# Transposing gathered rows one unit sooner, gathers ahead of scatters, column transfers in stage 3, and another order for the row tiles of a final norm

## The reference, cut to what matters

```
h = rmsnorm(x, norm_ffn_g) * (1 + sc2) + sh2
aff = softmax(h @ w_router)                       # 16 experts
gate, idx = top_k(aff.T, cap)                     # cap = 2 T / 16: 256 latent and 32 context tokens
xs = h[idx]
y  = (silu(xs @ w_e_gate[e]) * (xs @ w_e_up[e])) @ w_e_down[e]     # 1024 wide, per expert
x += gt2 * scatter_add(y * gate)
y_prompt, y_sample = rmsnorm(x, norm_final_g)
```

## Time and profile before

| what | value |
|---|---|
| median of 3 runs | 2752.36 us (2743.16 to 2754.95) |
| the profiled execution | 2750.49 us |
| its span, first to last instruction | 2748.7 us |
| TensorE matmuls busy | 2464.9 us, 90% |
| DVE, ACT, POOL busy | 59%, 44%, 28% |
| mean granted TensorE clock | 0.924 of full |
| chain that ended last | PE 63%, DVE 10%, ACT 9%, issue 6%, DMA 3% |
| start of expert 1 and of expert 14 on TensorE | 1529.6 and 2541.46 us |

### The profile page before, as it was taken

The page is one execution under the profiler, slowest core; times in us unless marked ns, Lnnn a source line. Parts: engine busy times, 40 slices in busy tenths (PEclk is TensorE's granted clock), DMA queues, the critical chain, the costliest instruction groups (busy, mean ns, idle before and its releaser), DMA issues.

```text
span 2748.7 us, 41035 instructions
## 1 busy us (share of the span) xinstructions
PE 2464.9 (90%) x15405; PEld 2165.3 (79%) x15405; DVE 1633.1 (59%) x2729; ACT 1214.1 (44%) x1952; POOL 762.4 (28%) x686
## 2 busy tenths in 40 slices
PE   5579999999997888999549999999999999999886
PEld 2568878687885567667219999999999999999886
DVE  1576959497694443341364666665566666655485
ACT  3555453455423223323115455555444555555473
POOL 1020110102000021101012544444445544444443
PEclk9889989999997888889659999999999999999998
DMA  5875465656637433422644666656666666566793
GB/s 204 301 271 184 165 227 191 230 184 210 203 110 239 136 112 126 147 83 99 108 99 140 200 190 187 184 182 200 203 192 200 202 180 190 181 193 198 248 311 149
DMA packets 287075, 505.63 MB, mean 184 GB/s; under 512 B 31614, under 2 KB 230107, under 8 KB 271098
## 3 DMA queue, kind: packets, MB, share of 16 engines
q1 hardware_dynamic: 247562, 377.84, 41.9%
q0 software_dynamic: 39408, 126.38, 16.4%
HBM read 405.63 MB, written 98.53 MB: 183 GB/s over the span
## 4 chain that ended last, share of the span: by engine, by line
PE 63%; DVE 10%; ACT 9%; issue 6%; DMA 3%; POOL 2%; DVEq 0%; SPq 0%; ACTq 0%; POOLq 0%
PE bank L1405 18%; PE bank L1407 17%; PE bank L1406 17%; DVE hl_exp L2372 2%; ACT hl_exp L1021 2%; ACT work_exp L1037 2%; DVE work_exp L2382 2%; PE bank L1588 1%; PE bank L1526 1%; PE bank L1619 1%; PE bank L1654 1%; PE bank L1553 1%; DVE work_out L2061 1%; PE bank L1565 1%; DMA raw_exp<-in_w_mod_dram 1%
## 5 line engine op out<-in xcount | busy, mean ns | idle before, releaser
L1405 PE MATMUL bank<-act_hl_exp,hl_exp 128*128 128x288 f32 x3072 | 914.7, 298 | 59.6 <-POOL act_hl_exp L1335 24.5
L1406 PE MATMUL bank<-act_hl_exp,hl_exp 128*128 128x288 f32 x3072 | 909.7, 296 | 0.0
L1407 PE MATMUL bank<-act_hl_exp,hl_exp 128*128 128x288 f32 x3072 | 908.0, 296 | 0.0
L1405 PEld LDWEIGHTS bank<-act_hl_exp,hl_exp 128*128 128x128 f32 x3072 | 579.5, 189 | 66.4 <-issue 46.9
L1407 PEld LDWEIGHTS bank<-act_hl_exp,hl_exp 128*128 128x128 f32 x3072 | 581.7, 189 | 0.0
L1406 PEld LDWEIGHTS bank<-act_hl_exp,hl_exp 128*128 128x128 f32 x3072 | 580.5, 189 | 0.0
L2372 DVE TENSOR_TENSOR hl_exp<-work_exp,hl_exp 128x1024 fp32r<-128x1024 f32 x192 | 237.3, 1256 | 224.1 <-ACT hl_exp L1021 223.9
L2372 DVE TENSOR_TENSOR hl_exp<-raw_exp,hl_exp 128x1024 fp32r<-128x1024 f32 x192 | 237.4, 1253 | 200.9 <-ACT hl_exp L1021 200.9
L2014 DVE SCALAR_TENSOR_TENSOR work_proj<-work_proj,wcv 128x392 f32<-128x392 f32 (+11 forms) x600 | 343.1, 642 | 0.0
L1356 POOL DMA_INDIRECT x_rows<-work_exp x135 | 253.0, 1874 | 141.7 <-DVE work_exp L2403 105.2
L1021 ACT ACTIVATE hl_exp<-work_exp 128x1024 fp32r<-128x1024 f32 x192 | 199.3, 1054 | 191.2 <-PE bank L1407 191.2
(11 more groups left out here) (320 smaller groups left out, 3669.8 us busy)
## 6 DMA issues: line engine op xcount, KB each, us to landing
hl_proj<-park_w POOLq DMA_DIRECT2D x80, 1024.0 KB, 5.5
raw_exp<-in_w_e_gate_dram SPq DMA_DIRECT2D x32, 1024.0 KB, 5.7
raw_exp<-in_w_e_up_dram SPq DMA_DIRECT2D x32, 1024.0 KB, 5.7
work_exp<-in_w_e_gate_dram SPq DMA_DIRECT2D x32, 1024.0 KB
work_exp<-in_w_e_up_dram SPq DMA_DIRECT2D x32, 1024.0 KB, 7.6
raw_exp<-in_w_e_down_dram SPq DMA_DIRECT2D x32, 1024.0 KB, 5.7
work_exp<-in_w_e_down_dram SPq DMA_DIRECT2D x32, 1024.0 KB, 5.4
park_w<-hl_proj SPq DMA_DIRECT2D x10, 2048.0 KB, 12.1
```

The costliest lines, as they stand in the source:

```text
L1405: pe.matmul(out, lh, rh, start=first, stop=False)
L1406: pe.matmul(out, lh, rl, start=False, stop=False)
L1407: return pe.matmul(out, ll, rh, start=False, stop=last_)
```

## The change

It has five parts.

- Stage 3's SP program issues the four column transfers after the first tile of block m = 2; they are gone from the start of routing.
- In an expert, gather_T and modulate_xe of column groups 0 to 7 stand in units 6 to 9; xe_hi stays in units 7 to 10, ahead of that unit's modulate_xe. gate_cols goes ahead of elo in unit 0.
- POOL's order in an expert is gather(e+2), scatter(e), xe_lo(e+2). In experts 13 and 14, outside the loop, a scatter waits for one block of out_rows at a time, and expert 13's scatter stays ahead of the gather.
- TensorE's units 0 and 1 wait for one transpose per bank, not two per unit.
- Final norm: rows are asked for after units 8 and 9; squares, roots, normalising and stores get other units; tiles 10 to 17 are loaded after expert 14's scatter has landed, come after the three `fix` tiles in the order (place), and are stored after the fixed rows have been scattered.

```diff
+        FIX, LAST = 10, NTILE + 3
+        def place(t):
+            return t if t < FIX else t + 3
...
+        f_s3 = Sig(k_m, 0, 0, 33)
...
                 if m > 0:
                     tile_out(G3[m] - 1)
+                if m == 2:
+                    for i, cols in ((1, A2), (2, mod[:, 24:32, :])):
+                        for cnd in range(2):
+                            sp.dma_start(mod_d[i, cnd].rearrange("(k p) -> p k", p=128), cols[:, :, cnd],
+                                         allow_slow_non_contiguous=True).then_inc(e_mod.sem, 16)
...
-            for i, cols in ((1, A2), (2, mod[:, 24:32, :])):
-                for cnd in range(2):
-                    sp.dma_start(mod_d[i, cnd].rearrange("(k p) -> p k", p=128), cols[:, :, cnd],
-                                 allow_slow_non_contiguous=True).then_inc(e_mod.sem, 16)
...
             def load_again(n):
-                sp.wait_ge(f_st[n % 2], 32 * (n // 2 + 1))
+                if n == 0:
+                    sp.wait_ge(e_sc, 16 * NB * (NE - 1))
+                if n % 2 == 0:
+                    sp.wait_ge(f_st[n // 2], 64)
...
+            STORE_AT = {15: (0,), 17: (1,), 18: (2, 3), 19: (4,), 20: (5, 6), 21: (7,), 22: (8, 9)}
             for u in range(2 * NEXP):
                 expert_units(NE - 2 + u // NEXP, range(u % NEXP, u % NEXP + 1))
-                if u in (7, 8):
-                    load_rows(u - 7)
-                if 12 <= u < 16:
-                    load_again(u - 12)
-                if 11 <= u < 16:
-                    store_pair(u - 11)
+                if u in (8, 9):
+                    load_rows(u - 8)
+                for t in STORE_AT.get(u, ()):
+                    store_tile(t)
                 if 19 <= u < 23:
-                    store_pair(u - 14)
+                    load_again(u - 19)
...
-            for q in range(2):
-                sp.wait_ge(f_st[q], STORED[q])
+            sp.wait_ge(f_wr, 48)
+            for t in range(FIX, NTILE):
+                store_tile(t)
+            upto(sp, f_s3, 16 * (NTILE - 8))
...
+            SQUARES_AT = {7: (0, 1), 8: (1, 3), 9: (3, 5), 10: (5, 6), 11: (8, 10), 18: (10, 12), 19: (12, 14), 20: (14, 18)}
+            ROOTS_AT = {9: (0, 5), 11: (5, 10), 19: (10, 14), 20: (14, 18)}
...
                     if 7 <= j < 11 and not last:
                         for k in (2 * (j - 7), 2 * (j - 7) + 1):
+                            xe_hi(e + 1, k)
+                    if 6 <= j < 10 and not last:
+                        for k in (2 * (j - 6), 2 * (j - 6) + 1):
                             modulate_xe(e + 1, k)
-                        for k in (2 * (j - 7), 2 * (j - 7) + 1):
-                            xe_hi(e + 1, k)
...
+            def gather_next(e, n_ids):
+                pool.wait_ge(e_gat, 16 * NB * e + 16 * NB)
+                pool.wait_ge(e_xk, 8 * e + 8)
+                pool.wait_ge(e_gate, e + 1)
+                gather(e + 1, n_ids)
+
+            def scatter(e, n_ids):
                 wait_pos(pool, e_sc, 16 * NB * e)
...
+                if isinstance(e, int):
+                    for n in range(2 if e == NE - 2 else 0):
                         upto(pool, f_x[n], 16 * (LOADS[n + 1] - LOADS[n]) + (16 if n == 0 else 0))
+                else:
+                    wait_alone(pool, s_alone, e_yev, NB * e + NB)
                 for b in range(NB):
+                    if isinstance(e, int):
+                        pool.wait_ge(e_yev, NB * e + b + 1)
...
+            gather_next(0, 1)
+            next_lo(0)
             with pool.Fori(0, NE - 3) as i:
-                expert(i + 1, False)
-            expert(NE - 2, False)
+                gather_next(i + 1, 2 * i + 2)
+                scatter(i, 2 * i + 3)
+                next_lo(i + 1)
+            scatter(NE - 3, 2 * NE - 4)
+            gather_next(NE - 2, 2 * NE - 3)
+            next_lo(NE - 2)
+            scatter(NE - 2, 2 * NE - 2)
...
-                                pe.wait_ge(e_yt, 8 * before + (2 * j + 2))
+                                pe.wait_ge(e_yt, 8 * before + (2 * j + q + 1))
...
-            NORM_PAIR = {6: 0, 7: 1, 8: 2, 9: 3, 10: 4, 13: 5, 14: 6, 15: 7, 16: 8}
+            TILES_AT = {10: (0,), 12: (1,), 13: (2, 3), 14: (4,), 15: (5, 6), 16: (7,), 17: (8, 9), 20: (10, 11), 21: (12, 13),
+                        22: (14, 15, 16), 23: (17,)}
...
+                    if j == 0:
+                        gate_cols(e)
                     if more and j != 7 and j != 11:
                         elo(e, j + 2)
-                    if j == 0:
-                        gate_cols(e)
...
-                    if 7 <= j < 11 and not last_e:
-                        gather_T(e + 1, 2 * (j - 7))
-                        gather_T(e + 1, 2 * (j - 7) + 1)
+                    if 6 <= j < 10 and not last_e:
+                        gather_T(e + 1, 2 * (j - 6))
+                        gather_T(e + 1, 2 * (j - 6) + 1)
+                    for t in TILES_AT.get(u + j, ()) if u is not None else ():
+                        norm_rows(place(t), 128, row_tile(t))
```

More of the change, by code:

```diff
@@ L1063, in squares @@
                 for t in range(t0, t1):
-                    square(t, 128, row_tile(t), 0, D, sq6[:, t:t + 1])
+                    c = place(t)
+                    square(c, 128, row_tile(t), 0, D, sq6[:, c:c + 1])
             def roots(t0, t1):
-                upto(act, f_sq, t1)
-                act.activation(rt6[:, t0:t1], sq6[:, t0:t1], ACT.Sqrt, bias=eps[:, :],
-                               scale=1.0 / D).then_inc(f_rt.sem, t1 - t0)
-            def norms(at):
-                if at in (4, 5):
-                    squares(3 * at - 12, 3 * at - 9)
-                if at == 5:
-                    roots(0, 6)
-                if at in (6, 7):
-                    squares(2 * at - 6, 2 * at - 4)
-                if at == 7:
-                    roots(6, 10)
-                if 11 <= at < 15:
-                    squares(2 * at - 12, 2 * at - 10)
-                if at == 12:
-                    roots(10, 14)
-                if at == 14:
-                    roots(14, 18)
+                a, z = place(t0), place(t1 - 1) + 1
+                upto(act, f_sq, z)
+                act.activation(rt6[:, a:z], sq6[:, a:z], ACT.Sqrt, bias=eps[:, :], scale=1.0 / D).then_inc(f_rt.sem, z - a)
+            SQUARES_AT = {7: (0, 1), 8: (1, 3), 9: (3, 5), 10: (5, 6), 11: (8, 10), 18: (10, 12), 19: (12, 14), 20: (14, 18)}
+            ROOTS_AT = {9: (0, 5), 11: (5, 10), 19: (10, 14), 20: (14, 18)}
+            def norms(at):
                 if at == 17:
@@ L1089, in norms @@
                     fix_roots()
+                if at in SQUARES_AT:
+                    squares(*SQUARES_AT[at])
+                if at == 10:
+                    squares(6, 8)
+                if at in ROOTS_AT:
+                    roots(*ROOTS_AT[at])
             def fix_squares():
@@ L1093, in fix_squares @@
                 for i, n in ROWS:
-                    t = NTILE + i
-                    square(t, n, fix[:, i, :], 0, D, sq6[0:n, t:t + 1])
+                    c = FIX + i
+                    square(c, n, fix[:, i, :], 0, D, sq6[0:n, c:c + 1])
             def fix_roots():
                 for i, n in ROWS:
-                    t = NTILE + i
-                    upto(act, f_sq, t + 1)
-                    act.activation(rt6[0:n, t:t + 1], sq6[0:n, t:t + 1], ACT.Sqrt, bias=eps[0:n, :],
+                    c = FIX + i
+                    upto(act, f_sq, c + 1)
+                    act.activation(rt6[0:n, c:c + 1], sq6[0:n, c:c + 1], ACT.Sqrt, bias=eps[0:n, :],
                                    scale=1.0 / D).then_inc(f_rt.sem, 1)
@@ L1336, in xe_lo, with next_lo @@
                     .then_inc(e_xlo, 1)
-            def expert(e, last):
-                if not last:
-                    pool.wait_ge(e_gat, 16 * NB * e + 16 * NB)
-                    pool.wait_ge(e_xk, 8 * e + 8)
-                    pool.wait_ge(e_gate, e + 1)
-                    gather(e + 1, 2 * e + 1)
-                    for k in range(KC):
-                        xe_lo(e + 1, k)
-                if last:
-                    return
+            def gather_next(e, n_ids):
[4 more added lines that the diff above has]
+            def scatter(e, n_ids):
                 wait_pos(pool, e_sc, 16 * NB * e)
                 pool.tensor_copy(ids_s[:, :], ids[:, e, :]).then_inc(e_ids, 1)
-                wait_alone(pool, s_alone, e_ids, 2 * e + 2)
-                if isinstance(e, int) and e == NE - 2:
-                    for n in range(4):
+                wait_alone(pool, s_alone, e_ids, n_ids)
+                if isinstance(e, int):
+                    for n in range(2 if e == NE - 2 else 0):
                         upto(pool, f_x[n], 16 * (LOADS[n + 1] - LOADS[n]) + (16 if n == 0 else 0))
-                wait_alone(pool, s_alone, e_yev, NB * e + NB)
+                else:
+                    wait_alone(pool, s_alone, e_yev, NB * e + NB)
```

(5 more changed lines are left out.)

25 lines of the change are left out of this document (10 added, 15 removed).

## The result

Two results have to be told apart. Where the change was timed first (call that chip A; its number is not on record) the kernel before took 2747.76 us in the median of its 4 runs and the changed one 2711.96 us (2708.22 to 2719.40), a ratio of 0.9867 [0.9841, 0.9893]; the forecast was 2707, with 2693 to 2722. Where both were run once more at the end (chip D) the changed kernel took 2743.56 us (12 runs) against 2751.43 (29 runs): 0.9984 [0.9963, 1.0004], no change that can be measured, and outside the range of the forecast. The first profile is read here; what chip D shows comes with its experiment.

What follows compares the result with a forecast made beforehand. TensorE, busy nine tenths of the span, was taken as the bound, so only its standing time could be saved; 2750.49 - 11.3 - 15.3 - 19.0 = 2704.9, plus 1.9 to the median of runs, gave 2707 us, range 2693 to 2722.

Steps and rivals of the forecast that it cites:

- Part 1, the columns: Start of routing: moving the column transfers to stage 3 ends TensorE's wait for the first w_mod block, -11.3 us.
- Part 2, the boundaries: Boundaries between experts: earlier gather_T and modulate_xe remove TensorE's 1.09 us loss at fourteen boundaries, -15.3 us.
- the finer wait: TensorE at expert boundaries: waiting for one transpose, not two, gives 0.36 us that nothing needs any more.
- so no cost of the branch shows: Expert loop: the gap is 0.94 us with the branch and 0.93 past the loop's end, so no branch cost.
- The rival that takes the branch: Expert loop: the branch keeps the gap, at most 1.09 us twelve times, +13.1, 2720 us; chance 0.14.
- Part 3, POOL: POOL in each expert: gathers before scatters, with 10 us of cover before xe_lo is due; price 0.
- Part 4, expert 14: Expert 14: rows asked for earlier end ACT's 15.11 us wait; 83.95 us instead of 103.0, -19.0 us.
- The four steps of the 7.2 us: End of expert 14: late ehi(12), elo, one tile and a transpose start expert 15 6.5 us late; slower clock adds 0.7.
- Part 5, expert 15 and the tail: Expert 15 and tail: moved stores and row loads cost 0, staying 77.6 and 26.6 us; bounds 0 and +15.
- 8 us more than the loads take: Expert 15: weights behind SP's wait for expert 14's scatter are wanted 42 us in, leaving 8 us of cover.
- the DMA engines bound expert 15: Rival in expert 15: row tiles, stores and weights fill the DMA engines, 2715 to 2722 us; chance 0.18.
- The slower rival, POOL falling behind: Every expert: scatters ending past T+54.7 delay xe_lo and the next expert, time over 2766 us; chance 0.03.

## Why the prediction was right, and where it was not

On chip A the time lies in the range and most of the mechanisms are those laid out. On chip D the time, 2743.56 us, lies outside it, by the step named under part 2.

- *Part 1, the columns (-11.3).* Right: the wait for w_mod is gone, some 10.5 us by the kernel that moves them alone, and stage 3 pays nothing that can be told from its own spread, some 14 us between executions.
- *Part 2, the boundaries (14 x 1.09 = -15.3).* Right on chips A and B, and for the reason given: ehis 5.82 us apart instead of 6.65 (6.07 was laid out), no wait for the output transposes, 1.21 us an expert. That the finer wait is needed by nothing was right too. On chips C and D the step failed, in this sentence: the gap is 0.94 with the branch and 0.93 past the loop's end, "so no cost of the branch shows". Equal gaps said only that no cost shows while TensorE pauses there. The rival that takes the branch had one thing right, that the time would be lost in the twelve passes entered by the jump, but not the place in the pass nor the size. It took 1.09 us a pass as the most that could be hidden and made it 2720; in the traces it is 14.7 us over twelve passes on chip C and 27.7 on D. That the branch is the cause is not shown.
- *Part 3, POOL (0).* Right: with the old order the time is the same.
- *Part 4, expert 14 (-19.0: 83.95 us).* Right: expert 14 took 82.6 us. The four steps of the 7.2 us are all in the timeline: the late ehi(12), elo, the tile, one transpose. But the gain does not reach the end, since expert 15 takes it back: with the row tiles in their old order the whole expert stage is as long.
- *Part 5, expert 15 and the tail (0, up to +15).* This is the term that was mis-sized on every chip: +14.3 and +1.8 us on chip A. By the starts of expert 15's 576 matmuls in the two traces the 14.3 can be named: 7.6 us more in gaps between them, the four waits for converted weights; 2.9 us by 28 more matmuls that start 0.24 us apart and not 0.133, the lower of TensorE's two clock levels, which came after the two longest of these waits (granted clock 0.83 from 2660 to 2680); and 3.7 us by which the last transposes ended later behind the last matmul, since six row tiles stood in front of them. The step put "8 us more than the loads take" as cover behind the wait for the scatter; the wait that decides is another, that of SP for the landing of tile 7's store, 18.7 us, with the last weights and the last rows behind it. The rival "the DMA engines bound expert 15" had the right place, about the right price (+8 to +15) and part of the reason: the store takes so long while the DMA engines are full (share 1.00 from 2630 to 2647). But they are at 0.79 in the window in which TensorE waits longest, and the same transfers in another order, with ACT's squares a unit later, gave 6.5 us back on chip D. So what could be won back lay in the order on SP and ACT; how much the full DMA engines cost by themselves was not tested.
- *The sum.* 2707 against 2712 on chip A is partly luck: part 5 lost 16 us more than was taken, while stages 1 to 3 were 7.6 us shorter in that execution with no change in their arithmetic, parts 2 and 4 gave 3 us more and part 1 gave 1.2 less. The working also counts its chances twice: those of the single cases sum to 1.00, with 0.97 inside the range, and yet some 0.15 is said to be left out.
- *The slower rival, POOL falling behind.* It did not come. What took the gain away on chip D was not on the list at its true size or place.

## What to carry to other kernels

Two equal gaps, one with a suspected cost and one without, show only that the cost is not seen while the gap is there. They are no bound for what the loop loses once the gap is gone: here the gap was 1.09 us, and 2.3 us a pass were lost without it on one chip and nothing on another. Whether the gap had hidden that loss is not shown. A gain of about 1% that comes from letting TensorE run without any pause through a loop has to be timed on more than one chip. And on a queue that runs in order, look at what each wait for a landing holds: here one wait for one store held the weights of the last two units and the last rows for 18.7 us.

## What was not expected of the hardware

- One and the same kernel took 2712 us in the median in one batch and 2744 in another, on another chip as far as is known, while the kernel before it took 2748 to 2751 in all. The traces put 27.7 us of it into the twelve passes that are entered by a jump, 24.0 us of them gaps of TensorE without a recorded cause at about one place in the pass.
- No instruction packets are recorded in those passes, only in the first.
- Stage 3, whose arithmetic no kernel here changed, took 474.1 to 490.6 us in different executions.
